# Expert weights in pairs of tiles, 32768 bytes to a partition, with every second column of gate and up products

## The reference, cut to what matters

```python
xs = jax.vmap(lambda hb, ib: hb[ib])(h, idx)          # 16 experts x 64 tokens x 1024
a = jnp.einsum('becd,edf->becf', xs, w_gate)          # w_gate, w_up: 16 x 1024 x 2048
u = jnp.einsum('becd,edf->becf', xs, w_up)
ye = jnp.einsum('becf,efd->becd', jax.nn.silu(a) * u, w_down) * g[..., None]   # 16 x 2048 x 1024
return zeros.at[idx].add(ye)                          # 512 x 1024
```

## Time and profile before

| what | value |
|---|---|
| time, median of 3 runs | 1299.17 us (1297.36 to 1302.92) |
| time of the profiled execution | 1296.7 us |
| its span, first to last instruction | 1294.7 us |
| PE busy | 1192.9 us, 92% of the span |
| DMA | 455.98 MB, mean 352 GB/s |
| TensorE clock granted | 0.997 of full speed |

### The profile page before, as it was taken

How to read it: one execution, slowest core, us unless ns; L and a number is a source line. 1 busy time by engine, 2 the same in 40 slices (tenths; PEclk the granted TensorE clock), 3 DMA queues, 4 the chain that set the end, 5 groups by cost and what they waited for, 6 DMA issues and landing times.

```text
span 1294.7 us, 12923 instructions
## 1 busy us (share of the span) xinstructions
PE 1192.9 (92%) x5378; PEld 501.9 (39%) x5378; DVE 342.1 (26%) x625; ACT 164.3 (13%) x350; POOL 33.8 (3%) x61
## 2 busy tenths in 40 slices
PE   5899999999989999999979899998979898888997
PEld 2444454554444353353324253342324234232332
DVE  3775829346450020210201121010201110020140
ACT  2510020034420001000100010000101000000021
POOL 2000020000000001000000000000000000000000
PEclk9999999999999999999999999999999999999999
DMA  9966320306469999999999999999999999999997
GB/s 347 401 227 239 132 82 0 131 1 260 197 247 386 426 429 420 429 428 428 427 428 429 428 427 427 429 428 428 428 429 428 429 428 429 428 428 428 426 427 319
DMA packets 44867, 455.98 MB, mean 352 GB/s; under 512 B 6208, under 2 KB 6320, under 8 KB 16922
## 3 DMA queue, kind: packets, MB, share of 16 engines
q1 hardware_dynamic: 44098, 454.95, 84.2%
q0 software_dynamic: 464, 0.33, 0.1%
q10 hardware_dynamic: 264, 0.11, 0.1%
HBM read 453.02 MB, written 2.36 MB: 352 GB/s over the span
## 4 chain that ended last, share of the span: by engine, by line
PE 64%; DMA 29%; DVE 4%; ACT 1%; issue 1%; SPq 1%; POOL 0%; DVEq 0%; POOLq 0%
DMA ring<-in_w_exp_up 27%; PE B L1259 17%; PE B L1223 14%; PE B L775 6%; PE B L1166 4%; PE B L1022 4%; PE B L903 3%; PE B L1276 3%; PE B L968 2%; DMA ring<-in_pos 2%; PE B L825 2%; PE B L1240 1%; PE B L1176 1%; PE B L1003 1%; PE B L891 1%
## 5 line engine op out<-in xcount | busy, mean ns | idle before, releaser
L1223 PE MATMUL B<-ring,moe 128*64 128x512 f32 x2016 | 448.5, 595 | 64.5 <-DMA ring<-in_w_exp_up 34.8
L1223 PEld LDWEIGHTS B<-ring,moe 128*64 128x64 f32 x2016 | 139.5, 137 | 367.6 <-issue 250.3
L1259 PE MATMUL B<-ring,moe 128*64 128x512 f32 x992 | 217.0, 594 | 0.4 <-issue 0.3
L2219 DVE TENSOR_TENSOR moe<-moe,B 128x512 f32<-128x512 f32 x30 | 19.8, 684 | 611.5 <-PE B L1223 611.5
L1259 PEld LDWEIGHTS B<-ring,moe 128*64 128x64 f32 x992 | 69.8, 137 | 133.3 <-issue 131.1
L775 PE MATMUL B<-ring 128*128 128x512 f32 x192 | 83.6, 594 | 0.0
L1609 ACT ACTIVATE moe<-B 128x512 f32<-128x512 f32 x32 | 17.4, 594 | 385.2 <-PE B L1223 385.2
L1276 PE MATMUL B<-moe 128*128 128x512 f32 x128 | 63.1, 618 | 0.5
L1166 PE MATMUL B<-moe,xl 128*128 128x128 f32 x448 | 56.7, 287 | 1.9 <-DVE moe L2198 1.9
L1166 PEld LDWEIGHTS B<-moe,xl 128*128 128x128 f32 x448 | 55.5, 201 | 2.2 <-DVE moe L2198 2.2
L775 PEld LDWEIGHTS B<-ring 128*128 128x128 f32 x192 | 36.1, 190 | 45.1 <-issue 45.1
(11 more groups left out here) (383 smaller groups left out, 794.8 us busy)
## 6 DMA issues: line engine op xcount, KB each, us to landing
ring<-in_w_exp_up SPq DMA_DIRECT2D x63, 2048.0 KB, 30.0
ring<-in_w_exp_gate SPq DMA_DIRECT2D x63, 2048.0 KB, 28.4
ring<-in_w_exp_down SPq DMA_DIRECT2D x61, 2048.0 KB, 33.9
ring<-in_w_in SPq DMA_DIRECT2D x6, 2048.0 KB, 9.3
ring<-in_w_mod SPq DMA_DIRECT2D x10, 1024.0 KB, 7.5
ring<-in_w_mod SPq DMA_DIRECT2D x4, 2048.0 KB, 14.4
fr<-in_w_mod SPq DMA_DIRECT2D x6, 1024.0 KB, 9.4
ring<-in_w_out SPq DMA_DIRECT2D x2, 2048.0 KB, 7.8
```

The source lines that it names most:

```text
L1223: x = mm(B[2 * up + n // 2][rows, :], xst[:, 2 * q + k, CAP * e2:CAP * (e2 + 1)], w[:, k, n * CH:(n + 1) * CH], start=(q == 0 and k == 0), ...
L1259: x = mm(B[5][CAP * half:CAP * (half + 1), :], hdt[:, q // 2, k * P + at:k * P + at + CAP], wd[:, k, half * CH:(half + 1) * CH], start=(q ...
L2219: v.tensor_tensor(hid[:, m, :], sil[:, m, :], B[2 + m][:, :], ALU.mult).then_inc(S["v_hid"], 1)
```

## The change

The expert weights of groups 1 to 7, and the first six tiles of the last expert, are loaded two tiles at a time: one DMA of 4 MB into two neighbouring slots, after PE has used both of their tiles (`expert_pair`). A partition then reads 32768 bytes in one piece: four rows of gate or up, eight rows of down. Group 0 and the last six tiles still come as single tiles, 16384 bytes to a partition, taken from every second such stretch.

For that the tiles are used in the order gate 0, gate 1, up 0, up 1, gate 2, gate 3, up 2, up 3 and down 0 to 3 (`FIRST_TILES` keeps the old order for the first expert), the slots are renumbered so that pairs are neighbours (`SLOT_OF`), and PE waits once for a pair. Because a partition now holds four neighbouring rows of gate and up, the token columns are taken by fours (`quad_rows` in place of `pair_rows`), for the router and the vectors of the norm too. Because it holds eight rows of down, the gate and up products read every second column of a tile: even columns into the lower half of the array, odd ones into the upper half. The order of the initial loads changes with the slots. For the last expert, `scatter` and the products of line 1377 are spread between the gate and up products.

```diff
-        SLOT_OF = [3, 7, 6, 5, 0, 1, 4, 2]
+        SLOT_OF = [6, 7, 4, 5, 0, 1, 2, 3]
...
         for e2 in range(2):
-            for q in range(4):
-                TILES += [("g", 4 * e2 + q), ("u", 4 * e2 + q)]
+            for q in (0, 2):
+                TILES += [(kind, 4 * e2 + q + n) for kind in "gu" for n in range(2)]
...
+            def expert_pair(i, group, after=0):
+
+                kind, st = TILES[i]
+                e2, q = divmod(st, 4)
+                r = (ring_turn(i, False) - after * HALF) % NSLOT
+                at = SLOT_OF[r] * SLOTF
+                dst = ring[:, at:at + 2 * SLOTF]
+                ex = expert(group, e2, after)
+                if kind == "d":
+                    src = A["w_exp_down"][0, bass.ds(ex, 1), (q // 2) * 2 * CH:(q // 2 + 1) * 2 * CH, :]
+                    src = src.rearrange("o (p k) n -> p (o k) n", p=P)
+                    dst = dst.rearrange("p (k n) -> p k n", k=8)
+                else:
+                    w = A["w_exp_gate" if kind == "g" else "w_exp_up"]
+                    src = w[0, bass.ds(ex, 1), (q // 2) * 4 * P:(q // 2 + 1) * 4 * P, :]
+                    src = src.rearrange("o (p k) n -> p (o k) n", p=P)
+                    dst = dst.rearrange("p (k n) -> p k n", k=4)
+                sp.dma_start(dst, src).then_inc(d_ring[r], 16)
...
             for n, i in enumerate(in_ring):
                 used(i, 0)
                 if n + NSLOT < len(in_ring):
                     expert_tile(in_ring[n + NSLOT], 0)
+                elif n % 2:
+                    expert_pair(n - 1 + NSLOT - len(in_ring), 1)
+            with sp.Fori(1, ALONE - 1) as j:
+                for i in range(0, NTI, 2):
+                    used(i + 1, j)
+                    expert_pair((i + NSLOT) % NTI, j if i + NSLOT < NTI else j + 1)
...
+                def products(kind, q):
+
+                    up = kind == "u"
+                    w = ring_tile(kind, 4 * e2 + q, group, after, first).rearrange("p (k n) -> p k n", k=2)
+                    for k in range(2):
+                        for n in range(4):
+                            rows = slice(CAP, P) if n % 2 else slice(0, CAP)
+                            x = mm(B[2 * up + n // 2][rows, :], xst[:, 2 * q + k, CAP * e2:CAP * (e2 + 1)],
+                                   w[:, k, (n // 2) * 2 * CH + n % 2:(n // 2 + 1) * 2 * CH:2],
+                                   start=(q == 0 and k == 0), stop=(q == 3 and k == 1))
+                    x.then_inc(S["p_gu"], 1)
...
+                for n, (kind, st) in enumerate(TILES[0:8]):
...
+                    products(kind, st)
+                    if last and n < NLT:
+                        scatter(group - 1, after, (2 * n, 2 * n + 1))
+                    elif last and n < 2 * NLT - 1:
+                        last_rows(n - NLT)
...
                             x = mm(B[5][CAP * half:CAP * (half + 1), :],
-                                   hdt[:, q // 2, k * P + at:k * P + at + CAP],
+                                   hdt[:, q // 2, (2 * (q % 2) + k // 2) * P + CAP * (k % 2):(2 * (q % 2) + k // 2) * P + CAP * (k % 2) + CAP],
                                    wd[:, k, half * CH:(half + 1) * CH],
...
             gate_up(NGROUP - 1, 0, 1, False, True)
-            pe.wait_ge(S["v_yacc"], 8 * (NGROUP - 1))
-            for c in range(NLT):
-                if c == 2:
-                    turn(NGROUP - 1, 0, 1, 0)
-                for half in range(2):
-                    x = mm(B[5][CAP * half:CAP * (half + 1), :], peq[:, c, 0:CAP], y3[:, c, half * CH:(half + 1) * CH],
-                           start=(c == 0), stop=False)
-            x.then_inc(S["p_tail"], 1)
+            last_rows(NLT - 1).then_inc(S["p_tail"], 1)
+            turn(NGROUP - 1, 0, 1, 0)
             turn(NGROUP - 1, 0, 1, 1)
```

More of the change, by code:

```diff
@@ L438, in expert_tile @@
             def expert_tile(i, group, after=0, last=False):
-                kind, st = TILES[i]
+                first = isinstance(group, int) and group == 0
+                kind, st = (FIRST_TILES if first else TILES)[i]
                 e2, q = divmod(st, 4)
-                first = isinstance(group, int) and group == 0
                 r = (ring_turn(i, first) - after * HALF) % NSLOT
@@ L467, in used @@
                 else:
-                    sp.wait_ge(S["p_gu"], 16 * group + (2 * st - 8 * after + (1 if kind == "g" else 2)))
+                    sp.wait_ge(S["p_gu"], 16 * group + (8 * (e2 - after) + at + 1))
             for n in range(len(LOADS)):
@@ new lines, in _ @@
+            for i in range(0, NTI, 2):
+                used(i + 1, ALONE - 1)
+                if i + NSLOT < NTI:
+                    expert_pair(i + NSLOT, ALONE - 1)
+                else:
+                    expert_pair(HALF + i + NSLOT - NTI, ALONE, 1)
+            for i in range(HALF, NTI, 2):
+                used(i + 1, ALONE, 1)
+                expert_pair((i + NSLOT) % NTI, ALONE if i + NSLOT < NTI else ALONE + 1, 1)
+            with sp.Fori(ALONE + 1, NGROUP - 2) as j:
+                for i in range(0, NTI, 2):
+                    used(i + 1, j, 1)
+                    expert_pair((i + NSLOT) % NTI, j if i + NSLOT < NTI else j + 1, 1)
@@ L536, in _ @@
+            for i in range(0, NTI, 2):
+                t = i + NSLOT - NTI
+                if t < SINGLE_FROM:
+                    used(i + 1, NGROUP - 2, 1)
+                    expert_pair((i + NSLOT) % NTI, NGROUP - 2 if t < 0 else NGROUP - 1, 1)
+                    continue
+                for n in range(2):
+                    used(i + n, NGROUP - 2, 1)
+                    expert_tile(t + n, NGROUP - 1, 1)
             for i in range(HALF - NSLOT):
@@ L1188, in ring_tile @@
                 n, r = divmod(ring_turn(i, first) - after * HALF, NSLOT)
-                pe.wait_ge(d_ring[r], NTI // NSLOT * 16 * group + 16 * (n + 1))
+                if first or r % 2 == 0:
+                    pe.wait_ge(d_ring[r], NTI // NSLOT * 16 * group + 16 * (n + 1))
+                elif isinstance(group, int) and group == NGROUP - 1 and i >= SINGLE_FROM:
+                    singles = len(range(r, NTI - len(OWN_HOME), NSLOT))
+                    pe.wait_ge(d_ring[r], 16 * (singles + 1))
                 return slot(SLOT_OF[r])
@@ L1198, in gate_up @@
             def gate_up(group, e2, after, first=False, last=False):
-                for q in range(4):
-                    wg = ring_tile("g", 4 * e2 + q, group, after, first).rearrange("p (k n) -> p k n", k=2)
-                    if first and e2 == 0:
+                def products(kind, q):
[8 more added lines that the diff above has]
+                    x.then_inc(S["p_gu"], 1)
+                if first and e2 == 0:
+                    for q in range(4):
                         if q == 0:
```

105 lines of the change are left out of this document (42 added, 63 removed).

## The result

The changed kernel takes 1323.94 us (median of 4 runs, 1322.69 to 1325.58) against 1298.74 us for the kernel before in the same series: a ratio of 1.0189, 95% interval 1.0163 to 1.0215. That is 25.2 us more, where 3.8 us less was forecast, and 20 us above the end of the range. The profiled execution has a span of 1322.1 us, 27.4 more than before.

What follows compares the result with a forecast made beforehand. The prediction took the DMA rate as the bound, with PE alone until nearly 600 us. Its terms, -5.8 + 2.5 + 0 + 0 - 0.5 = -3.8 us, gave 1295.4 us against the median 1299.17; range 1288 to 1304.

Steps and rivals of the forecast that it cites:

- the order and the strided reads: Gather and gate/up products: gather by fours costs 0.2 us a group, hidden; strided products taken as costing nothing.
- the moving read: Gate/up products reading every second column: taken as 0, up to 67 ns an instruction hidden; other end 204 / 140.
- The spare: In each expert, PE needs 50.1 of 58.74 us, leaving 8.6 us to hide extra PE work.
- The rule: SBUF reads: two hits per 16-byte line give full bandwidth; fours should be slower than twos, products by twos free.
- rival (c): Strided gate/up products: 27.47 us become 40.0, the DMA no longer sets the pace, about 1412 us; chance 0.09.
- The longer pieces: Weight loads in 32 KB pieces: 0.075 us saved per pair, 77 pairs, -5.8 us; bounds 0 and 12.1.
- The coarser refill: Pairs issued only after both tiles are used: DMA hole at the turn from group 0 to 1, +2.5 us.
- Group 3: Pair refill between the last up tile and down there: some 2 us to spare, so 0, bound 2.
- The tail: Last expert to the end: 1.0 us gained, of which 0.5 counts: -0.5 us, bounds 0 and 1.
- Rival (d): PE's clock falls after 2.9 us waits for pairs: 5.4 us hidden, only 2 us in group 3 would cost; chance 0.03.

Runs made afterwards that it cites:

- e4: Kernel before, with its gather reading token columns by fours: 1310.50 us, ratio 1.0097.
- e1: Changed kernel, with its gather reading token columns by twos again: 1302.74 us, ratio 1.0036.
- e2: Changed kernel, with gate and up products reading plain neighbouring columns: 1319.28 us, ratio 1.0166.
- e11: Changed kernel, both strides kept, with group 1 loaded tile by tile: 1324.96 us, ratio 1.0205.
- e3: Changed kernel, with the gather by twos again and the products reading plain columns: 1298.75 us, ratio 1.0004.
- e6: e3 with the order of the kernel before at the last expert: 1298.71 us, ratio 1.0003.
- e5: Kernel before, with gather loads at steps of 1 to 8 floats and products at 1 to 4: 1442.40 us, run once.
- e7: e3 with each pair issued as two 2 MB transfers of 16 KB pieces: 1301.29 us, ratio 1.0020.
- e8: e6 with group 1 refilled and waited for tile by tile, pairs from group 2 on: 1297.88 us, ratio 0.9992.
- e9: e8 with everything tile by tile from tile 18 of group 7 on, the whole last expert included: 1295.75 us, ratio 0.9981.

## Why the prediction was wrong

**The step that failed** is in the part on the order and the strided reads: "Taking columns by fours instead of twos makes the gather's loads those of line 1240: 204 instead of 201 ns, 64 x 0.003 = 0.2 us in a group, within the spare 8.6." Both halves of it were wrong.

*The neighbour.* Line 1240 is a transpose, line 1166 a product, and the loads of the two differ at every step. The kernel before has a transpose of the same tokens that the gather reads, by twos:

```profile
L1074 PEld LDWEIGHTS B<-cst_sb,xl 128*128 128x128 f32 x32 | 4.3, 210 | 1.1 <-DVE xl L1689 0.5 <-issue 0.5
```

A transpose's load takes 140 ns plain, 210 by twos, and 204 to 216 by fours (L1240, L1106, L1286). Sixteen of them take 2.07 us by twos and 2.09 by fours, so step 4 costs nothing over step 2. A product's load takes 192 ns plain, 196 to 201 by twos, and 328 or 329 by fours. That 201 and 204 lay so close together was chance: the one is a product by twos, the other a transpose by fours. A row with the same tile shape, 128x128 floats, was taken for a row with the same price. The bound from the other side that the same paragraph used for the moving read (204 / 140) was not even asked for here. The block of 32 went from 3.77 to 7.46 us: 7.4 us a group and 7.0 at the first gather, where 0.2 stood.

*The spare.* 8.6 us an expert is read between 910 and 969 us. The first paragraph of the prediction says itself that the chain is PE alone until nearly 600 us, and the earlier trace rows has 386 and 426 there: the DMA waits for slots that PE has not given back. Whatever PE does ahead of the last such gap costs in full. How much of it arrives is read from the landing of one and the same tile, the last up tile of group 2. It is where the load in each of these lines of the chains ends (start plus length): the kernel before, e4, e1.

```profile
642.07 32.41 DMA ring<-in_w_exp_up
```

```profile
663.04 25.63 DMA ring<-in_w_exp_up
```

```profile
651.75 28.17 DMA ring<-in_w_exp_up
```

In the kernel before, the gather by fours delays this tile by 688.67 - 674.48 = 14.2 us. In the changed kernel, set beside e1, it delays it by 694.76 - 679.92 = 14.8 us. Both come to what two gathers cost PE, 7.0 + 7.4 = 14.4 us: the two that lie ahead of the gaps of 494 to 516 us; the third, at about 590 us, is followed by no gap of weight and adds next to nothing. At the last up tile of the expert before the last the two parts differ: 1218.80 - 1204.73 = 14.1 us in the kernel before, 1227.41 - 1206.36 = 21.1 in the changed kernel. The 6 us more are the gap of group 3 (128 GB/s from 788 to 798 us), less what little there is of it in e1. That is most of what turns 12.3 (e4) into 21.2 (e1). Every kernel that has both the gather by fours and pairs in group 3 shows that gap: 398 GB/s from 700 to 800 us in the changed kernel, 409 in e2, 405 in e11. None with one of them alone does: 428 in e4, 429 in e1, 428 in e3, 425 in e6. That it is the refill by pairs in group 3, and not another part of the change, fits SP's 33.3 us without an issue, but no run varies that refill alone.

**The rule.** The prediction set the rule of the Trainium skill (SBUF — State Buffer, Specifications) beside the row and gave it no rival with a price and a chance. It said of the rule that "columns by fours, one hit a line, should be slower than by twos, and the moving reads by twos should be free", and the first is what e1, e4 and e5 show, the second nearly so (225 ns in place of 215). The 3 ns that spoke against it came from another kind of instruction.

**The moving read**, "I take nothing": 10 ns of 215 each. The mechanism of rival (c), 204 / 140, is refuted (28.80 us, not 40.0), and 10 ns is well under the 67 said to be hidden. It costs 2.9 to 4.7 us all the same, by the same error on the spare: two experts' products, 2.7 us, lie ahead of the gap at 500 us, and with the slow gather the gap of group 3 adds to it.

**The longer pieces**, -5.8 us: the rate was right, and that all of it arrives at the end is not shown (2.3 us between e7 and e3). 432 GB/s (431.6 forecast), 58.1 to 58.3 us an expert (58.3 forecast), 1214 ns a piece (1215). In e3, whose first gather starts 4.6 us later than before (391.67 against 387.08), the last up pair of the expert before the last lands 2.2 us later: 2.4 ahead in all. The later start is left out of the account, for this execution is 3.2 us above the median of e3.

**The coarser refill**, +2.5: right in e3 (2.0 us at 500 to 560), though closing it in e8 brought 0.8 at most. In the changed kernel the hole of "495 to 499 us" became one of 8 us, since a gather twice as long lies ahead of the next used pair.

**Group 3**, 0 with a bound of 2: right in e3 (428 GB/s from 700 to 800), wrong in the changed kernel (398: 7.0 us), where the cover was gone, PE's two gather blocks being 7.4 us longer there.

**The tail**, -0.5: wrong sign. From the landing of the last up pair of the expert before the last, e3 needs 1299.9 - 1206.9 = 93.0 us and the kernel before 89.9: +3.1. The prediction had PE wait for loads in the last expert and counted 0.4 us for each fetch of rows. In e3 each fetch (L1282) takes 0.86 us, as it did before (two in 1.72 at line 1377), each of the four steps of the scatter between the first products (L1326) 1.91, and PE never waits. But the old order (e6) gives the same time, so the spread end as such is not what costs. With -2.4 ahead and +3.1 here e3 comes to +0.7; measured is +0.5.

**Rival (d), the clock:** the waits for a pair are there, and the falls too: 2.54 us of wait, then 8.78 in place of 7.09 us. Ahead of the last expert one is on the path, 1.7 us, which the prediction had as hidden.

## What to carry to other kernels

Price a strided operand by a row of the same kind of instruction with the same operand in that role; if there is none, keep both ends and give the documented rule a rival of its own. Before writing "within the spare", ask at which time the spare was read, and count what the engine does ahead of the last gap in the transfers: that arrives in full, even if the kernel waits for its loads in half of the span (from 591 to 1264 us here). And look at the longest stretch between two refills: a refill in larger units wins rate, but makes that stretch longer, and a slower engine can turn it into a gap. At the end it makes the last consumer wait for a larger unit; that issuing small again helps there is suggested by e9 and not shown beyond noise.

## What the runs showed of the hardware

- A float operand of TensorE's products at steps of 1, 2, 3 and 4 floats (e5, one execution): weight loads of 192, 196, 260 and 328 ns, moving reads of 215, 225, 339 and 455 ns an instruction of 512 columns; 317 to 335 ns for loads at 5 to 8.
- A transpose's load of 128x128 floats: 140 ns plain, 210 by twos, 204 to 216 by fours.
- Pieces of 32 KB in transfers of 4 MB go at 432 GB/s (e3), of 16 KB in transfers of 2 MB at 428 (e7).
- After 2.54 us of idle PE's next block of 32 took 8.78 in place of 7.09 us (e3); after 1.02 us it took 7.09. Not every such wait does this: in e1 a block of 32 with the products' stride took 7.42 us after 2.29 us of idle, and 9.03 in the changed kernel after 2.21. The granted clock from 1206 to 1216 us was 0.83, between the levels of 1.2 and 2.4 GHz as a mean:

```profile
1197.31 7.09 PE L1248 MATMUL B<-ring,moe 128*64 128x512 f32 x32 [1.02 <-DMA ring<-in_w_exp_gate]
1206.93 8.78 PE L1248 MATMUL B<-ring,moe 128*64 128x512 f32 x32 [2.54 <-DMA ring<-in_w_exp_up]
```
